# Expert weights of a decoder trunk loaded by halves of the rows for both experts of a pair

## The chip, the cores and the metric

The kernel runs on one core of one Trainium2 chip, in one launch. The metric is the device time of that core in microseconds (us); less is better. The kernel before takes 2008.51 us, the median of three runs (2006.98 to 2011.86).

## The reference

A trunk of two layers over 512 tokens of 1024 float32 numbers. Each layer first mixes (an attention with three branches, a state-space branch, gates and an output projection) and then sends each token through two of 32 experts. An expert is `(silu(x @ w_gate) * (x @ w_up)) @ w_down`, with `w_gate` and `w_up` of 1024 x 512 and `w_down` of 512 x 1024, each 2 MB:

```python
g_sel = argmax(h @ w_rg + b_rg)                     # one of 4 groups of experts
top_p, top_i = top_k(softmax(e_logits[g_sel]), 2)   # two experts in the group
w = g_w * top_p / sum(top_p)
for each expert e, xb its tokens:
    out = (silu(xb @ w_gate[e]) * (xb @ w_up[e])) @ w_down[e]
x = x + sum over both experts of w * out
```

All experts' weights are read in each layer: 96 matrices, 201 MB.

## The kernel before

One program with a stream for each engine; semaphores set the order. A layer has a mixing stage and an expert stage; the diff touches the second alone.

**Pairs.** The 32 experts are taken in 16 pairs. A pair's tokens, 64 places for either expert, are one tile of 128: `gather` (L519) fetches rows of the normalised tokens from `h_rows` in DRAM, `turn_rows` (L1011) transposes them, DVE's `gain_rows` (L1841) scales them into `xg`. A round of 16 pairs serves up to 64 tokens an expert; with these inputs a layer takes one round. `both` (L1018) writes the products of both experts of the pair to one PSUM bank, the first expert's to the upper 64 partitions, the second's to the lower: for each of 8 (for `down`: 4) blocks k of rows, one matmul for each expert. One of its calls shows in the trace as 32 records.

**A pair on TensorE** (`pair`, L1026): wait for the tokens; wait for both gate matrices (`landed`, L1030), 16 products to bank 2, `gate_free`; wait for both up matrices, 16 products to bank 3, `up_free`; transposes of the next pair's tokens; once ACT's silu (L1343) and DVE's product (`gated`, L1852) are done, four transposes to bank 6, which ACT copies to `actT` (L1345); wait for both down matrices, 8 products to bank 4 (`half_done`) and 8 to bank 5 (`down_free`). ACT copies both banks to `yslot` (L1348, L1350), and POOL scatters it to `y_rows` in DRAM (L524).

**Loads.** SP issues 96 loads of 2 MB a layer, one matrix of one expert each (`load`, L632), in the order gate, gate, up, up, down, down of each pair. They go to ten places (`slots`, L167), in turn; two of these are the tiles `hT` and `h`, one is `spare_slot`. On a partition a load is 16 KB in one piece, in DRAM too. Loads 0 and 1 are issued while attention runs, 2 to 5 at its end, 6 and 7 when the output projection is done, 8 and 9 when the first pair's token rows have landed (L658). From load 10 on, `refill` (L665) waits for the products that read the load ten before: that is `gate_free`, `up_free` or `down_free`, each counted once a pair.

**The end of a layer.** The last pair's results aren't scattered: TensorE multiplies `yslot` with a matrix of shares (L1074). When the pair before it has been scattered, SP reads all results back (`ytok`, L680: four loads of 1 MB, 8 KB a partition, to `h` and `hT`); DVE adds them to `x` (L1877, eight operations), then the last pair's (L1884, eight operations). The next layer, or the output, waits for that.

**The start of the expert stage.** ACT writes the normalised tokens to `h_rows` tile by tile (L1166); POOL waits for the last of the four and for the table of places (`table_ready`, L1812) and gathers the first pair's rows (L531). This releases TensorE and loads 8 and 9.

Of the kernel before, what the change touches and what calls it, by code (L numbers as in the profile page):

```python
# [24 lines left out]
P = 128  # L25
# [107 lines left out]
def trunk(nc, a, out):  # L133
    with ExitStack() as ctx:
# [39 lines left out]
        def uses(s):  # L174

            return len(range(s, LOADS, NSLOT))
# [4 lines left out]

        def slot_of(i):

            return slots[i % LOADS % NSLOT].rearrange("p (k n) -> p k n", k=KF if KINDS[i % 6 // 2] == "down" else KD)

        squares = view(100, D)
        xrow = view(96, D)
# [258 lines left out]
        def wait_reg(eng, s, value):  # L446

            eng.wait_ge(s, value)
            eng.sem_inc(tick, 1)
# [118 lines left out]
        def _(sp):  # L568
            for t in range(NT):
                sp.dma_start(x[:, t, :], a["x"][0][P * t:P * t + P, :]).then_inc(x_tile[t], 16)  # L570
            with sp.Fori(0, DEPTH) as l:
# [60 lines left out]
                def load(i, pair):  # L632

                    kind = KINDS[i % 6 // 2]
                    src = a["expert_" + kind][bass.ds(l * NE + 2 * pair + i % 2, 1), :, :]
                    sp.dma_start(slot_of(i), src.rearrange("o (p k) n -> p (o k) n", p=P))\
                      .then_inc(slot_in[i % LOADS % NSLOT], 16)

                def freed(i):
# [25 lines left out]
                def refill(j, base, pair):  # L665

                    i = j % LOADS
                    prev = last_load(i) if j >= LOADS else j - NSLOT
                    wait_reg(sp, freed(prev), base + (prev // 6 + 1))
                    load(i, pair)  # L670

                with sp.Fori(0, nb * (PAIRS // BODY) - 1) as q:
# [1 line left out]
                        refill(j, q * BODY, (q * BODY + j // 6) % PAIRS)  # L674
                for j in range(NSLOT, LOADS):
                    refill(j, earlier + (PAIRS - BODY), PAIRS - BODY + j // 6)
                wait_reg(sp, up_free, earlier + (PAIRS - 1))
                wait_reg(sp, y_out, earlier * 16 + 16 * (PAIRS - 1))
                for t in range(NT):
                    sp.dma_start(ytok[t], y_rows[2 * P * t:2 * P * t + 2 * P, :].rearrange("(p k) d -> p k d", k=2))\  # L680
                      .then_inc(y_tok[t], 16)
                wait_reg(sp, gate_free, earlier + PAIRS)
                leave(sp, left_exp)
            for t in range(NT):
                sp.wait_ge(x_tile[t], 16 * (DEPTH + 1))
# [11 lines left out]
        def _(pe):  # L697
# [308 lines left out]
            def experts():  # L1006
                pe.wait_ge(rounds_ready, 1)
                nb = pe.value_load(rounds[0:1, 0:1], min_val=1, max_val=MAXR)
                earlier = pe.value_load(rounds[0:1, 1:2], min_val=0, max_val=PAIRS * (MAXR - 1))

                def turn_rows():  # L1011
                    for k in range(KD):
                        r = pe.transpose(bank[:, k // 4, P * (k % 4):P * (k % 4) + P],
                                         xrow[:, P * k:P * k + P], ident[:, :])
                        if k % 4 == 3:
                            r.then_inc(xt_done, 1)

                def both(dst, moving, first, cols, n):  # L1018

                    for k in range(n):  # L1020
                        for e in range(2):
                            r = pe.matmul(dst[CAP * e:CAP * e + CAP, :], moving[:, k, CAP * e:CAP * e + CAP],  # L1022
                                          slot_of(first + e)[:, k, cols], start=(k == 0), stop=(k == n - 1))
                    return r

                def pair(pp, base, last):  # L1026

                    it = base + pp

                    def landed(first):  # L1030
                        for i in (first, first + 1):
                            s = i % NSLOT
                            wait_reg(pe, slot_in[s], base * (16 * uses(s) // BODY) + 16 * (i // NSLOT + 1))

                    wait_reg(pe, xg_ready, it * 2 + 3)
                    landed(6 * pp)
                    both(bank[:, 2, :], xg, 6 * pp, slice(0, FF), KD).then_inc(gate_free, 1)
                    landed(6 * pp + 2)
                    both(bank[:, 3, :], xg, 6 * pp + 2, slice(0, FF), KD).then_inc(up_free, 1)
                    if last:  # L1040

                        pe.wait_ge(shares_ready, 1)
                        for t in range(NT):
                            r = pe.transpose(bank[:, 7, P * t:P * t + P], share[:, t, :], ident[:, :])
                        r.then_inc(shares_turned, 1)
                    else:
                        wait_reg(pe, rows_in, it * 16 + 32)
                        turn_rows()
                    wait_reg(pe, act_ready, it + 1)
                    for f in range(KF):  # L1050
                        r = pe.transpose(bank[:, 6, P * f:P * f + P], hid[:, f:FF:KF], ident[:, :])  # L1051
                    r.then_inc(at_done, 1)
                    wait_reg(pe, at_ready, it + 1)
                    landed(6 * pp + 4)
                    for half in range(2):
                        wait_reg(pe, y_ready, it * 2 + (1 + half))
                        r = both(bank[:, 4 + half, :], actT, 6 * pp + 4, slice(512 * half, 512 * half + 512), KF)
                        if half == 0:
                            r.then_inc(half_done, 1)
                    r.then_inc(down_free, 1)  # L1060

                pe.wait_ge(rows_in, 16)
                turn_rows()
                with pe.Fori(0, nb * (PAIRS // BODY) - 1) as q:
                    for pp in range(BODY):
                        pair(pp, q * BODY, False)
                for pp in range(BODY):
                    pair(pp, earlier + (PAIRS - BODY), pp == BODY - 1)

                pe.wait_ge(shares_copied, 1)  # L1070
                for half in range(2):
                    wait_reg(pe, y_ready, earlier * 2 + (2 * PAIRS + 1 + half))
                    for t in range(NT):
                        pe.matmul(bank[:, (2 * t + 4 + half) % 8, :], shareT[:, t, :], yslot[:, 512 * half:512 * half + 512],  # L1074
                                  start=True, stop=True).then_inc(y_near, 1)
# [60 lines left out]
        def _(act):  # L1136
# [125 lines left out]
            for l in range(DEPTH):  # L1262
# [76 lines left out]
                act.sem_inc(y_ready, 2)  # L1339
                act.sem_inc(yslot_free, 1)  # L1340
                with act.Fori(0, nb * PAIRS) as it:
                    wait_reg(act, gate_free, it + 1)
                    act.activation(silu, bank[:, 2, :], ACT.Silu).then_inc(silu_done, 1)  # L1343
                    wait_reg(act, at_done, it + 1)
                    act.activation(actT.rearrange("p a b -> p (a b)"), bank[:, 6, :], ACT.Copy).then_inc(at_ready, 1)  # L1345
                    wait_reg(act, half_done, it + 1)
                    wait_reg(act, yslot_free, it + 1)
                    act.activation(yslot[:, 0:512], bank[:, 4, :], ACT.Copy).then_inc(y_ready, 1)  # L1348
                    wait_reg(act, down_free, it + 1)
                    act.activation(yslot[:, 512:1024], bank[:, 5, :], ACT.Copy).then_inc(y_ready, 1)  # L1350
                leave(act, left_exp)

# [2 lines left out]
        def _(dve):  # L1355
# [52 lines left out]
            for l in range(DEPTH):  # L1408
# [439 lines left out]

                def gated(it):
                    wait_reg(dve, silu_done, it + 1)  # L1850
                    wait_reg(dve, up_free, it + 1)
                    TT(hid, silu, bank[:, 3, :], ALU.mult).then_inc(act_ready, 1)  # L1852

                with dve.Fori(0, earlier + (PAIRS - 1)) as it:
# [3 lines left out]
                        gain_rows(q)  # L1858

                late = Chain(dve, exp_chain)  # L1860
                wait_reg(dve, down_free, earlier + (PAIRS - 1))
                for t in range(NT):
                    for k, dst in enumerate((share, share_b)):
                        late(TS(dst[:, t, :], iota_f[:, :], place[:, B_, t, k:k + 1], w_near[:, t, k:k + 1],
# [49 lines left out]
```

## Time and profile before

| | us |
|---|---|
| median of 3 runs | 2008.51 |
| profiled execution, time | 2007.55 |
| its span | 2005.8 |
| PE busy | 1712.3 (85%) |
| DVE busy | 567.3 (28%) |
| ACT busy | 401.9 (20%) |
| DMA, mean over the span | 247 GB/s |
| mean granted TensorE clock | 0.946 |

Times in the rows are in us from the start of the span. In the chain of waits each piece is what the end waited for at that time. A releaser in brackets is what ended the engine's idle time. A load's landing is the last of its 16 engines' parts. A matmul takes two records here, and the two experts' matmuls overlap, so that 32 records take 7.1 us at the full clock.

### The profile page before, as it was taken

To read this page: it belongs to the slowest core of one execution; us is meant where nothing else is said; L and a number is where in the kernel's file an instruction comes from. 1 tells how busy PE (TensorE), PEld (TensorE's weight loads), DVE (VectorE), ACT (ScalarE), POOL (GpSimd) and SP (SyncE) were. 2 spreads that over 40 slices of the span, in tenths; PEclk is the share of its full clock that TensorE was granted. 3 is DMA by queue.
4 is the path that set the end of the run, shared out by engine and by line. 5 is a ranking of instruction groups with operands and counts; after the bars stand their busy time and mean duration, and the time that the engine had idled before them with its cause. 6 is when DMAs were issued, how large, how long until landed. Compare 5 with 4: busy or idle time off the path is not lost.

```text
span 2005.8 us, 21398 instructions
## 1 busy us (share of the span) xinstructions
PE 1712.3 (85%) x7534; PEld 811.0 (40%) x7534; DVE 567.3 (28%) x1748; ACT 401.9 (20%) x959; POOL 80.7 (4%) x153
## 2 busy tenths in 40 slices
PE   7969899999698778787899698999996988787877
PEld 6644344445333233332367343444452333232332
DVE  4753134524200000000356622345252000000003
ACT  2211334303111111101122113343031111111110
POOL 0000000000010000000000000000000000000000
PEclk9989899999799898999999798999997999998999
DMA  5720110152799999999929110102518999999996
GB/s 156 175 93 22 42 43 22 51 231 86 313 426 427 427 427 427 427 427 427 353 62 229 39 42 22 43 22 100 234 59 340 426 428 427 426 427 427 426 427 289
DMA packets 118707, 496.25 MB, mean 247 GB/s; under 512 B 40884, under 2 KB 77748, under 8 KB 93008
## 3 DMA queue, kind: packets, MB, share of 16 engines
q1 hardware_dynamic: 107968, 474.33, 59.4%
q0 software_dynamic: 8928, 16.39, 2.2%
q10 hardware_dynamic: 1712, 4.20, 0.5%
q8 instruction: 64, 1.05, 0.2%
q14 instruction: 35, 0.29, 0.0%
HBM read 488.99 MB, written 30.41 MB: 259 GB/s over the span
## 4 chain that ended last, share of the span: by engine, by line
PE 56%; DMA 31%; DVE 4%; ACT 4%; SPq 2%; issue 2%; POOL 0%; DVEq 0%; POOLq 0%; ACTq 0%
PE bank L1022 15%; PE bank L737 12%; DMA arena<-in_expert_up 12%; PE bank L716 11%; DMA arena<-in_expert_gate 8%; DMA arena<-in_expert_down 6%; PE bank L933 6%; PE bank L868 2%; DMA h<-in_expert_up 2%; PE bank L890 2%; PE bank L900 2%; PE bank L771 1%; SPq L573 1%; DMA h_rows<-h 1%; PE bank L853 1%
## 5 line engine op out<-in xcount | busy, mean ns | idle before, releaser
L1022 PE MATMUL bank<-arena 128*64 128x512 f32 x2240 | 604.7, 627 | 96.7 <-DMA arena<-in_expert_up 40.8
L1022 PEld LDWEIGHTS bank<-arena 128*64 128x64 f32 x2240 | 210.2, 144 | 367.2 <-issue 367.2
L737 PE MATMUL bank<-hT,arena 128*128 128x512 f32 x512 | 269.7, 625 | 46.2 <-ACT arena L1216 44.8
L1852 DVE TENSOR_TENSOR arena<-arena,bank 128x512 f32<-128x512 f32 x32 | 22.0, 688 | 840.2 <-PE bank L1022 840.2
L1022 PE MATMUL bank<-spare_slot,arena 128*64 128x512 f32 x320 | 155.6, 644 | 36.7 <-DMA arena<-in_expert_gate 14.3
L1022 PE MATMUL bank<-hT,arena 128*64 128x512 f32 x256 | 121.5, 631 | 28.9 <-DMA h<-in_expert_up 18.0
L737 PEld LDWEIGHTS bank<-hT,arena 128*128 128x128 f32 x512 | 84.6, 195 | 106.4 <-ACT arena L1216 55.2
L1022 PE MATMUL bank<-h,arena 128*64 128x512 f32 x256 | 121.8, 632 | 0.0
L933 PE MATMUL bank<-arena,hT 128*128 128x512 f32 x256 | 117.8, 612 | 4.2 <-DVE hT L1726 4.2
L716 PE MATMUL bank<-arena,hT 128*128 128x256 f32 (+1 forms) x512 | 115.5, 386 | 1.8 <-ACT h L1189 1.8
L1684 DVE TENSOR_REDUCE nbias<-bank 128x1 f32<-128x31 f32 (+4 forms) x192 | 63.4, 383 | 176.1 <-PE bank L871 95.9
L716 PEld LDWEIGHTS bank<-arena,hT 128*128 128x128 f32 x512 | 97.0, 191 | 17.0 <-ACT h L1189 2.2
L1343 ACT ACT_TABLE_LOAD x32 | 41.1, 1283 | 291.2 <-PE bank L1022 291.2
L1022 PEld LDWEIGHTS bank<-spare_slot,arena 128*64 128x64 f32 x320 | 45.8, 148 | 129.8 <-issue 129.8
L716 PE MATMUL bank<-arena 128*128 128x512 f32 (+1 forms) x208 | 84.7, 567 | 6.0 <-ACT arena L1193 4.9
L1236 ACT ACTIVATE arena<-bank,nbias 128x31 f32<-128x31 f32 (+4 forms) x192 | 82.6, 439 | 8.1 <-DVE nbias L1684 8.1
L1345 ACT ACTIVATE arena<-bank 128x512 f32<-128x512 f32 x32 | 19.1, 597 | 310.4 <-PE bank L1051 310.4
L1022 PEld LDWEIGHTS bank<-hT,arena 128*64 128x64 f32 x256 | 36.1, 145 | 102.7 <-issue 102.7
L933 PEld LDWEIGHTS bank<-arena,hT 128*128 128x128 f32 x256 | 48.0, 195 | 57.9 <-issue 51.9
L1246 ACT ACTIVATE arena<-bank 128x512 f32<-128x512 f32 (+1 forms) x64 | 38.0, 594 | 154.4 <-PE bank L890 154.4
L890 PE MATMUL bank<-ident,arena 128*128 128x128 f32 (+1 forms) x384 | 62.0, 280 | 1.6 <-DVE arena L1699 0.9
L716 PEld LDWEIGHTS bank<-arena 128*128 128x128 f32 (+1 forms) x208 | 37.5, 185 | 53.6 <-issue 46.8
(345 smaller groups left out, 1604.7 us busy)
## 6 DMA issues: line engine op xcount, KB each, us to landing
arena<-in_expert_gate SPq DMA_DIRECT2D x48, 2048.0 KB, 36.9
arena<-in_expert_down SPq DMA_DIRECT2D x48, 2048.0 KB, 38.9
arena<-in_expert_up SPq DMA_DIRECT2D x44, 2048.0 KB, 36.8
arena<-in_w_in SPq DMA_DIRECT2D x26, 1024.0 KB, 8.4
spare_slot<-in_expert_gate SPq DMA_DIRECT2D x8, 2048.0 KB, 30.8
hT<-in_expert_up SPq DMA_DIRECT2D x8, 2048.0 KB, 36.8
h<-in_expert_up SPq DMA_DIRECT2D x8, 2048.0 KB, 42.3
spare_slot<-in_expert_down SPq DMA_DIRECT2D x8, 2048.0 KB, 37.5
```

What stands on the lines that cost most here:

```text
L716: r = pe.matmul(dst, w, m, start=(i == 0), stop=(i == len(pairs) - 1))
L737: r = pe.matmul(bank[:, FB, :], lhs, rhs, start=(k == 0), stop=last)
L868: pe.matmul(bank[:, i, 0:nk], qT[rows, g, P * qt:P * qt + P], keys[rows, :], start=True, stop=False)
L890: r = pe.transpose(bank[0:w, 4 + kt % 2, P * i:P * i + P], prob[:, n % 2, i, P * kt:P * kt + w], ident[:, :])
L900: r = pe.matmul(bank[DH * j:DH * j + DH, 6, 0:2 * P], v, pT[0:w, c % 4, :].rearrange("p (g j t) -> p j g t", g=2, j=2)[:, j], start=(br == ...
L933: r = pe.matmul(bank[:, c, :], mergedT[:, k, P * t:P * t + P], w_o[:, k, 512 * c:512 * c + 512], start=(k == 0), stop=(k == KD - 1))
L1022: r = pe.matmul(dst[CAP * e:CAP * e + CAP, :], moving[:, k, CAP * e:CAP * e + CAP], slot_of(first + e)[:, k, cols], start=(k == 0), stop=( ...
L1236: act.activation(prob[:, n % 2, i, 0:nk], bank[:, i, 0:nk], ACT.Exp, scale=-1.0, bias=nbias[:, n % 2, i:i + 1], accum_out=rsum[:, n % 2, i ...
L1246: act.activation(pT[0:w, c % 4, :], bank[0:w, 4, :], ACT.Copy).then_inc(evac_act, 1)
L1343: act.activation(silu, bank[:, 2, :], ACT.Silu).then_inc(silu_done, 1)
L1684: dve.tensor_reduce(nbias[:, n % 2, i:i + 1], bank[:, i, 0:nk], AX.X, ALU.min).then_inc(max_ready, 1)
L1852: TT(hid, silu, bank[:, 3, :], ALU.mult).then_inc(act_ready, 1)
```

## The change

A load brings half the rows of one matrix, for both experts of the pair, in place of one expert's whole matrix. The place then holds, on each partition, 8 KB of the first expert and 8 KB of the second (`slot_of`). `both` does half of the blocks k for one load, with both experts in turn as before; TensorE waits for one load, multiplies, reports and waits for the next. `gate_free`, `up_free` and `down_free` count twice a pair, and all that wait for them count so too. For `down`, the first half goes to banks 4 and 5, then the second half to both. Order, number and size of the loads, and the ten places, stay.

```diff
--- before.py
+++ after.py
@@ -181,7 +181,8 @@
 
         def slot_of(i):
 
-            return slots[i % LOADS % NSLOT].rearrange("p (k n) -> p k n", k=KF if KINDS[i % 6 // 2] == "down" else KD)
+            return slots[i % LOADS % NSLOT].rearrange("p (e k n) -> p e k n", e=2,
+                                                      k=(KF if KINDS[i % 6 // 2] == "down" else KD) // 2)
 
         squares = view(100, D)
         xrow = view(96, D)
@@ -632,8 +633,9 @@
                 def load(i, pair):
 
                     kind = KINDS[i % 6 // 2]
-                    src = a["expert_" + kind][bass.ds(l * NE + 2 * pair + i % 2, 1), :, :]
-                    sp.dma_start(slot_of(i), src.rearrange("o (p k) n -> p (o k) n", p=P))\
+                    src = a["expert_" + kind][bass.ds(l * NE + 2 * pair, 2), :, :].rearrange("o (p k) n -> p o (k n)", p=P)
+                    n = KD * FF // 2
+                    sp.dma_start(slot_of(i).rearrange("p e k n -> p e (k n)"), src[:, :, n * (i % 2):n * (i % 2) + n])\
                       .then_inc(slot_in[i % LOADS % NSLOT], 16)
 
                 def freed(i):
@@ -666,7 +668,7 @@
 
                     i = j % LOADS
                     prev = last_load(i) if j >= LOADS else j - NSLOT
-                    wait_reg(sp, freed(prev), base + (prev // 6 + 1))
+                    wait_reg(sp, freed(prev), base * 2 + (prev // 6 * 2 + prev % 2 + 1))
                     load(i, pair)
 
                 with sp.Fori(0, nb * (PAIRS // BODY) - 1) as q:
@@ -674,12 +676,12 @@
                         refill(j, q * BODY, (q * BODY + j // 6) % PAIRS)
                 for j in range(NSLOT, LOADS):
                     refill(j, earlier + (PAIRS - BODY), PAIRS - BODY + j // 6)
-                wait_reg(sp, up_free, earlier + (PAIRS - 1))
+                wait_reg(sp, up_free, earlier * 2 + 2 * (PAIRS - 1))
                 wait_reg(sp, y_out, earlier * 16 + 16 * (PAIRS - 1))
                 for t in range(NT):
                     sp.dma_start(ytok[t], y_rows[2 * P * t:2 * P * t + 2 * P, :].rearrange("(p k) d -> p k d", k=2))\
                       .then_inc(y_tok[t], 16)
-                wait_reg(sp, gate_free, earlier + PAIRS)
+                wait_reg(sp, gate_free, earlier * 2 + 2 * PAIRS)
                 leave(sp, left_exp)
             for t in range(NT):
                 sp.wait_ge(x_tile[t], 16 * (DEPTH + 1))
@@ -1015,28 +1017,29 @@
                         if k % 4 == 3:
                             r.then_inc(xt_done, 1)
 
-                def both(dst, moving, first, cols, n):
-
-                    for k in range(n):
+                def both(dst, moving, i, cols, n):
+
+                    for k in range(n // 2 * (i % 2), n // 2 * (i % 2 + 1)):
                         for e in range(2):
                             r = pe.matmul(dst[CAP * e:CAP * e + CAP, :], moving[:, k, CAP * e:CAP * e + CAP],
-                                          slot_of(first + e)[:, k, cols], start=(k == 0), stop=(k == n - 1))
+                                          slot_of(i)[:, e, k % (n // 2), cols], start=(k == 0), stop=(k == n - 1))
                     return r
 
                 def pair(pp, base, last):
 
                     it = base + pp
 
-                    def landed(first):
-                        for i in (first, first + 1):
-                            s = i % NSLOT
-                            wait_reg(pe, slot_in[s], base * (16 * uses(s) // BODY) + 16 * (i // NSLOT + 1))
+                    def landed(i):
+                        s = i % NSLOT
+                        wait_reg(pe, slot_in[s], base * (16 * uses(s) // BODY) + 16 * (i // NSLOT + 1))
 
                     wait_reg(pe, xg_ready, it * 2 + 3)
-                    landed(6 * pp)
-                    both(bank[:, 2, :], xg, 6 * pp, slice(0, FF), KD).then_inc(gate_free, 1)
-                    landed(6 * pp + 2)
-                    both(bank[:, 3, :], xg, 6 * pp + 2, slice(0, FF), KD).then_inc(up_free, 1)
+                    for i in (6 * pp, 6 * pp + 1):
+                        landed(i)
+                        both(bank[:, 2, :], xg, i, slice(0, FF), KD).then_inc(gate_free, 1)
+                    for i in (6 * pp + 2, 6 * pp + 3):
+                        landed(i)
+                        both(bank[:, 3, :], xg, i, slice(0, FF), KD).then_inc(up_free, 1)
                     if last:
 
                         pe.wait_ge(shares_ready, 1)
@@ -1051,13 +1054,15 @@
                         r = pe.transpose(bank[:, 6, P * f:P * f + P], hid[:, f:FF:KF], ident[:, :])
                     r.then_inc(at_done, 1)
                     wait_reg(pe, at_ready, it + 1)
-                    landed(6 * pp + 4)
-                    for half in range(2):
-                        wait_reg(pe, y_ready, it * 2 + (1 + half))
-                        r = both(bank[:, 4 + half, :], actT, 6 * pp + 4, slice(512 * half, 512 * half + 512), KF)
-                        if half == 0:
-                            r.then_inc(half_done, 1)
-                    r.then_inc(down_free, 1)
+                    for i in (6 * pp + 4, 6 * pp + 5):
+                        landed(i)
+                        for half in range(2):
+                            if i % 2 == 0:
+                                wait_reg(pe, y_ready, it * 2 + (1 + half))
+                            r = both(bank[:, 4 + half, :], actT, i, slice(512 * half, 512 * half + 512), KF)
+                            if i % 2 and half == 0:
+                                r.then_inc(half_done, 1)
+                        r.then_inc(down_free, 1)
 
                 pe.wait_ge(rows_in, 16)
                 turn_rows()
@@ -1339,14 +1344,14 @@
                 act.sem_inc(y_ready, 2)
                 act.sem_inc(yslot_free, 1)
                 with act.Fori(0, nb * PAIRS) as it:
-                    wait_reg(act, gate_free, it + 1)
+                    wait_reg(act, gate_free, it * 2 + 2)
                     act.activation(silu, bank[:, 2, :], ACT.Silu).then_inc(silu_done, 1)
                     wait_reg(act, at_done, it + 1)
                     act.activation(actT.rearrange("p a b -> p (a b)"), bank[:, 6, :], ACT.Copy).then_inc(at_ready, 1)
                     wait_reg(act, half_done, it + 1)
                     wait_reg(act, yslot_free, it + 1)
                     act.activation(yslot[:, 0:512], bank[:, 4, :], ACT.Copy).then_inc(y_ready, 1)
-                    wait_reg(act, down_free, it + 1)
+                    wait_reg(act, down_free, it * 2 + 2)
                     act.activation(yslot[:, 512:1024], bank[:, 5, :], ACT.Copy).then_inc(y_ready, 1)
                 leave(act, left_exp)
 
@@ -1848,7 +1853,7 @@
 
                 def gated(it):
                     wait_reg(dve, silu_done, it + 1)
-                    wait_reg(dve, up_free, it + 1)
+                    wait_reg(dve, up_free, it * 2 + 2)
                     TT(hid, silu, bank[:, 3, :], ALU.mult).then_inc(act_ready, 1)
 
                 with dve.Fori(0, earlier + (PAIRS - 1)) as it:
@@ -1858,7 +1863,7 @@
                         gain_rows(q)
 
                 late = Chain(dve, exp_chain)
-                wait_reg(dve, down_free, earlier + (PAIRS - 1))
+                wait_reg(dve, down_free, earlier * 2 + 2 * (PAIRS - 1))
                 for t in range(NT):
                     for k, dst in enumerate((share, share_b)):
                         late(TS(dst[:, t, :], iota_f[:, :], place[:, B_, t, k:k + 1], w_near[:, t, k:k + 1],
```

## Rows read from the trace of the kernel before

**Rows 1.** The page: how much the core's DMA engines moved, in 40 slices of the span.
```profile
GB/s 156 175 93 22 42 43 22 51 231 86 313 426 427 427 427 427 427 427 427 353 62 229 39 42 22 43 22 100 234 59 340 426 428 427 426 427 427 426 427 289
```

**Rows 2.** The page, section 4: shares of the chain that ended last, by line.
```profile
PE bank L1022 15%; PE bank L737 12%; DMA arena<-in_expert_up 12%; PE bank L716 11%; DMA arena<-in_expert_gate 8%; DMA arena<-in_expert_down 6%; PE bank L933 6%; PE bank L868 2%; DMA h<-in_expert_up 2%; PE bank L890 2%; PE bank L900 2%; PE bank L771 1%; SPq L573 1%; DMA h_rows<-h 1%; PE bank L853 1%
```

**Rows 3.** Chain of waits, experts of the first layer: start, length in us, what.
```profile
525.93 15.83 PE bank L1022 x64
...
947.37 9.87 PE bank L1022 x32
...
980.71 14.02 DMA hT<-y_rows
...
999.96 0.66 DVE x L1884
```

**Rows 4.** Chain of waits, end of the second layer's experts.
```profile
1939.57 43.88 DMA arena<-in_expert_down
...
1983.97 8.70 PE bank L1022 x32
```

**Rows 5.** DVE timeline at both ends: start, us, line, [idle before <-releaser].
```profile
989.44 5.12 DVE L1877 SCALAR_TENSOR_TENSOR x<-h,w_far,x 128x1024 f32<-128x1024 f32 x4 [2.14 <-DMA h<-y_rows]
...
1985.96 5.12 DVE L1877 SCALAR_TENSOR_TENSOR x<-h,w_far,x 128x1024 f32<-128x1024 f32 x4 [3.70 <-DMA h<-y_rows]
1991.00 5.12 DVE L1877 SCALAR_TENSOR_TENSOR x<-hT,w_far,x 128x1024 f32<-128x1024 f32 x4
1996.15 0.69 DVE L1884 TENSOR_TENSOR x<-x,bank 128x512 f32<-128x512 f32 x1
1997.26 4.28 DVE L1884 TENSOR_TENSOR x<-x,bank 128x512 f32<-128x512 f32 x7 [0.43 <-PE bank L1074]
```

**Rows 6.** DMA view of the load issued at 944.05: KB, us to landing.
```profile
arena<-in_expert_down SPq DMA_DIRECT2D x1, 2048.0 KB, 42.9
```

**Rows 7.** DMA view, 560 to 960 us: packets, MB, share of 16 engines.
```profile
DMA packets 15082, 170.81 MB, mean 427 GB/s; under 512 B 3344, under 2 KB 3344, under 8 KB 5094
...
q1 hardware_dynamic: 11219, 163.42, 96.0%
```

**Rows 8.** DMA view, 984 to 990 us, tokens' rows come back (8 KB packets).
```profile
DMA packets 346, 2.54 MB, mean 423 GB/s; under 512 B 40, under 2 KB 40, under 8 KB 40
...
q1 hardware_dynamic: 345, 2.53, 100.5%
```

**Rows 9.** DMA view, 396 to 400 us, halves of w_out's rows (2 KB packets).
```profile
DMA packets 784, 1.59 MB, mean 398 GB/s; under 512 B 6, under 2 KB 6, under 8 KB 784
```

**Rows 10.** DMA view of three loads, issued at 523.12, 535.28 and 535.90.
```profile
h<-in_expert_up SPq DMA_DIRECT2D x1, 2048.0 KB, 13.4
...
spare_slot<-in_expert_down SPq DMA_DIRECT2D x1, 2048.0 KB, 8.3
...
arena<-in_expert_down SPq DMA_DIRECT2D x1, 2048.0 KB, 12.6
```

**Rows 11.** DMA view of the second layer's same places, issued at 1519.92 and 1532.02.
```profile
h<-in_expert_up SPq DMA_DIRECT2D x1, 2048.0 KB, 12.9
...
spare_slot<-in_expert_down SPq DMA_DIRECT2D x1, 2048.0 KB, 8.2
```

**Rows 12.** DMA view of two writes to h_rows, issued at 508.91 and 493.56.
```profile
h_rows<-h ACTq DMA_DIRECT2D x1, 512.0 KB, 9.3
...
h_rows<-h ACTq DMA_DIRECT2D x1, 512.0 KB, 3.1
```

**Rows 13.** Timeline ahead of the first gather.
```profile
515.92 0.23 DVE L1812 TENSOR_SCALAR table<-table 128x128 int32<-128x128 int32 x1
...
519.15 1.23 POOL L521 DMA_INDIRECT arena<-h_rows,table  x1 [434.53 <-DMA h_rows<-h]
```

**Rows 14.** PE timeline, two groups of the last pair, each after a landing.
```profile
1963.35 8.76 PE L1022 MATMUL bank<-arena 128*64 128x512 f32 x32 [2.03 <-DMA arena<-in_expert_gate]
...
1973.73 7.09 PE L1022 MATMUL bank<-arena 128*64 128x512 f32 x32 [1.62 <-DMA arena<-in_expert_up]
```

## The prediction, made before the changed kernel was run

> **What bounds the kernel now.** I read the strip of what the DMA engines moved first [rows 1]: both expert stages, slices 12 to 18 and 32 to 39, stand at 426 to 428 GB/s and nothing else does. Then the shares of the chain [rows 2]: the three expert matrices' DMAs make 26% of it beside 15% for the products of L1022. So in the expert stage loads set the pace; TensorE waits for them. Two things follow. Places that come free earlier are worth something only where DMA engines have nothing queued, and products that begin earlier only where the end waits for products.
>
> Where does the end wait? The chain of the first layer's end goes back from DVE's last additions to the read-back of the tokens' rows at 980.71 [rows 3]. The second layer's shows a down load that lands at 1939.57 + 43.88 = 1983.45 and then 8.70 us of products [rows 4]; the naive reading is that halves save half of that. I therefore looked at DVE beside it [rows 5]. Its eight operations L1877 begin when the first read-back lands, 1985.96, take 10.2 us, and L1884 follows at 1996.15 with next to no gap: only 1997.26 - 1996.15 - 0.69 = 0.42 us of the tail is due to late products. In the first layer DVE begins at 989.44, and from 999.96 on it waits for no product. The read-back stands in SP's queue behind the last load: that one lands at 944.05 + 42.9 = 986.95 [rows 6] and the first read-back 2.5 us later, in the second layer 1983.45 and 1985.96, again 2.5 us, the time that 1 MB takes at 427 GB/s. So each layer ends 2.5 + 10.2 + 5 us after its last load lands (the products run beside that), and the place of the last landing is what the change can move.
>
> **The change part by part.**
>
> *Products by halves.* Same number of matmuls. In the last pair the products end earlier by about half a group, 3.5 us of 7.09 [rows 14], in up and in down alike. All but 0.42 us of it falls under DVE's tail. Worth -0.4 us in the second layer, 0 in the first. The cover is DVE's tail: if the read-back came earlier, this would begin to count.
>
> *The two waits more per group.* Chain pieces hold 64 records in 15.83 us across two such waits [rows 3], with a first group that starts at the low clock; a wait that is already met shows no gap. I take 0; even 0.3 us each would leave a pair at 24 + 2 us against the 6 x 5.2 = 31 us that its loads take.
>
> *Places free by halves: the gap at the start of the stage.* Load 9 is issued at 523.12 and lands 13.4 later, at 536.5; load 10 is issued at 535.28, once all 16 gate products are done, and lands at 543.6; load 11 lands at 548.5 [rows 10]. Loads that are queued land 4.9 us apart, these two 7.1: a gap of 2.2 us. In the second layer it is 1532.02 + 8.2 - (1519.92 + 12.9) = 7.4, a gap of 2.5 [rows 11]. After the change load 10 waits for half the gate products: these start at 525.93, and although their start is at the low clock (64 records in 15.83 us, less 7.1 for the second group, leaves 8.7 for the first), the second half is at the full clock, so the first is done 7.09 / 2 = 3.5 us before the whole. Load 10 is then issued near 531.8, before load 9 is through. The gap closes: -2.2 and -2.5 us, I take -2.35 a layer. Bounds 0 (load 10 is not early enough) and -2.5. After this PE needs less time for a pair than its loads do, the queue grows (at the end a load lands 42.9 us after its issue), and earlier issues change nothing.
>
> *Packets.* A load's 16 KB a partition were one packet and are now two of 8 KB. In 400 us of the stage 163.42 MB took 96.0% of 16 engines [rows 7]: 37.6 engine-us per MB, 0.616 us per 16 KB. The read-back has 8 KB packets: 2.53 MB in 100.5% of 96 engine-us, 38.1 per MB [rows 8]. That is 1.4% more by the shares and 0.95% by the rates (427 against 423). The stretch in which loads queue up is 986.9 - 543.6 = 443 us, 85 loads at 5.2. So +4.2 us a layer by the rates; bounds +2.2 (0.5%, as the views are rounded) and +6.2 (1.4%). It all is on the path, since the last landing sets the end. The Trainium skill, DMA: Bandwidth & Descriptors, "Why small descriptors are slow (HBM only)", gives a fixed cost of about 3 cycles per packet, at its 850 MHz 3.5 ns; 8 packets more per load and engine over 85 loads would be an estimated 2.4 us a layer. The rows give more (0.95% of 616 ns is 5.9 ns a packet), and I go by the rows.
>
> *The write of the last tile to h_rows.* It is issued at 508.91 while loads 6 and 7 run and takes 9.3 us; undisturbed it takes 3.1 [rows 12]. The gather of the first pair follows it at 519.15, though the table was ready at 515.92 + 0.23 = 516.15 [rows 13]. Engines take packets of two queues in turn, as far as the 9.3 us tell, so with 8 KB packets between them the 4 KB packets of the write get through sooner. At most the gather starts 1 us after the table (as it does after the write now), at 517.1: -2.0 us. At least 0: the total work of that moment is the same, and the slowest engine is nearly out of loads when it gets to the write. I take -0.8. The whole stage starts that much earlier. The same skill page, "Queues, rings and completion order", says that an engine goes round its queues packet by packet; the row of 9.3 against 3.1 agrees.
>
> *Issues.* 256 pieces instead of 128 per load may make each of SP's issues longer. The issues of 535.28 and 535.90 are 0.62 us apart, so one takes less than that now; with 5.2 us per load even twice as much is hidden, save ahead of loads 8 and 9: 0, bound +0.4.
>
> Sum a layer: -2.35 - 0.8 + 4.2 = +1.05; two layers +2.1, less 0.4 for the end: **+1.7 us**. On the profiled execution's 2007.55 that is 2009.3; it lies 0.96 below the median of the runs, so 2010.2 as a median. I say 2010. Bounds by these terms: low 2 x (-2.5 - 2.0 + 2.2) - 0.4 = -5; high 2 x (0 + 0 + 6.2 + 0.4) = +13.
>
> **The rivals.**
>
> *Faster (13%).* The packets cost next to nothing, since 16 engines are held by something else than the packet's own overhead, and both starts gain in full: 2 x (-2.5 - 2.0) - 0.4 = -9.4, 1999. If the products' halves also counted in the tail, 3.5 a layer, 1992. For it: the chain of the second layer does name the products. Against it: rows 5, and the 423 against 427.
>
> *Slower (15%).* At any time the engines now read one 8 KB half of each 16 KB, at two places 2 MB apart. If that is slower to read than 16 KB in one piece, the last landing moves by 4.4 us a layer for each per cent. It passes a measurable loss (+6) from 1.4 + 0.3 = 1.7% on, 420 GB/s. The nearest row with halves of rows is w_out's: 2 KB of each 4 KB, 398 GB/s [rows 9], 6.8% below; at that rate it is +32 a layer less 3, +58, 2066. But seven packets more per 16 KB at 5.9 ns each are 41 ns of 616, 6.7%: their number explains it, and nothing is left for the gaps between the pieces. I put this rival's middle at 2018. The skill's same page, "Latency and other measured facts", tells of copies with rows 512 KB to 8 MB apart that fall to half the rate; halving the rate for 443 us a layer would end near 2900. Rows lie 16 KB apart here, only the two experts lie 2 MB apart, and nothing in the trace has such a distance; I leave it 1 of the 15%.
>
> *TensorE's clock (7%).* After 2.03 us of idleness a group took 8.76 us, after 1.62 us 7.09 [rows 14]; 9.87 in another case [rows 3]. The waits before each half could leave TensorE at 1.2 GHz for as long as in the worst group now, 9.87 - 7.09 = 2.8 us more, in several halves. The last down products would then end where they do now or 2 to 3 us later, and DVE's last additions would wait for them: 2012 to 2015. For it: six waits a pair in place of three. Against it: each wait is shorter (5.2 less 3.5 us), and a TensorE that falls behind no longer waits.
>
> **How the numbers follow.** Forecast 65%, faster 13%, slower 15%, clock 7%. A measurement of this kernel tells about 0.3%, 6 us, from no change: 2002.5 to 2014.5. Of the forecast's 65 about 3 lie below (its low end and the runs' spread) and 4 above. Faster by over 0.3%: 0.13 + 0.03 = 0.16. Slower: 0.15 + 0.04 + 0.02 of the clock's = 0.21. The same: 0.63. The range, 2001 to 2021, takes in the forecast's bounds but for the last us or two and the slower case up to 0.6%.
>
> **What would show it.** Right: 49,000 packets of 8 KB in place of 24,600 of 16 KB; the stage's rate at 422 to 425 GB/s; loads 9 and 10 landing 5 us apart; the write of the last tile to h_rows at 7.5 to 9; PE's products of the last pair over 3 to 4 us earlier relative to the last landing, with DVE L1877 still beginning 2.5 us after it. Wrong: a rate of 427 (then faster) or under 421 (slower); a read-back that lands before the last load, or a gap between L1877 and L1884 that a product ends.

## The result, and the profile after

The changed kernel takes 2012.87 us (median of 20 runs, 2008.29 to 2018.35) against 2007.78 for the kernel before (20 runs, 2004.66 to 2011.86): ratio 1.0024, interval 1.0015 to 1.0032. That is 5.1 us more, a loss so small that it is inside what I had called "the same", and inside the range of 2001 to 2021; the forecast of 2010 had 1.7 us of loss. The profiled execution took 2009.47 us with a span of 2007.8, 3.4 us less than the median.

First the strips of the page [rows 1]. Each digit or number is one of 40 slices.

```profile
PEclk9989999999799999999999899999998999999999
...
GB/s 156 176 91 22 39 40 28 38 228 102 335 420 420 422 421 421 420 420 421 353 84 217 51 26 38 43 22 94 231 77 357 421 420 420 421 421 422 420 421 307
DMA packets 143281, 496.21 MB, mean 247 GB/s; under 512 B 40884, under 2 KB 77748, under 8 KB 93008
```

Both expert stages stand at 420 to 422 GB/s where they stood at 426 to 428, and the packets are 24,600 more. The DMA view of 560 to 960 us beside [rows 7]: 421 for 427.

```profile
DMA packets 24673, 168.35 MB, mean 421 GB/s; under 512 B 3270, under 2 KB 3270, under 8 KB 5002
```

The DMA view of single loads (KB, us to landing): load 9 of both layers, issued at 522.58 and 1519.87, load 10, at 531.11 and 1528.10, and the last load, at 952.80 and 1953.99 [rows 6, 10, 11].

```profile
h<-in_expert_up SPq DMA_DIRECT2D x1, 2048.0 KB, 13.0
...
h<-in_expert_up SPq DMA_DIRECT2D x1, 2048.0 KB, 13.3
...
spare_slot<-in_expert_down SPq DMA_DIRECT2D x1, 2048.0 KB, 10.0
...
spare_slot<-in_expert_down SPq DMA_DIRECT2D x1, 2048.0 KB, 10.8
...
arena<-in_expert_down SPq DMA_DIRECT2D x1, 2048.0 KB, 38.5
...
arena<-in_expert_down SPq DMA_DIRECT2D x1, 2048.0 KB, 32.9
```

The same two microseconds, 534 to 536, of the kernel before and of this one (after the engines' busy times: PEclk, DMA share, GB/s):

```profile
534.00:536.00 2.00, 2.00 (x12) 0.63 (x9) 0.00 (x0) 0.98 (x1) 0.00 (x0) 1.00 0.42 164
```

```profile
534.00:536.00 2.00, 2.00 (x12) 0.74 (x10) 0.00 (x0) 1.73 (x2) 0.00 (x0) 1.00 1.01 418
```

The hole ahead of load 10, in which the DMA engines were busy for 0.42 of the time, is filled. Loads 9 and 10 land at 535.6 and 541.1, 5.5 us apart in place of 7.1, and at 1533.2 and 1538.9, 5.7 in place of 7.4. The last load lands at 991.3 and 1986.9. From load 10 to the last it is 450.2 and 448.0 us, where it was 443.3 in both layers.

The last write to h_rows, issued at 509.28, and the first gather [rows 12, 13]:

```profile
h_rows<-h ACTq DMA_DIRECT2D x1, 512.0 KB, 8.4
```

```profile
518.59 1.23 POOL L522 DMA_INDIRECT arena<-h_rows,table  x1 [433.78 <-DMA h_rows<-h]
```

From the write's issue to the gather it is 9.31 us, before 519.15 - 508.91 = 10.24.

The end of the second layer. TensorE (start, us, line, [idle before <-releaser]):

```profile
1972.16 3.65 PE L1024 MATMUL bank<-arena 128*64 128x512 f32 x16 [1.89 <-DMA arena<-in_expert_up]
1977.13 3.65 PE L1024 MATMUL bank<-arena 128*64 128x512 f32 x16 [1.32 <-DMA arena<-in_expert_up]
...
1983.76 7.09 PE L1024 MATMUL bank<-arena 128*64 128x512 f32 x32 [1.26 <-ACT arena L1350]
1990.77 7.13 PE L1079 MATMUL bank<-arena,spare_slot 128*128 128x512 f32 x16
```

and DVE [rows 5]:

```profile
1989.34 5.12 DVE L1882 SCALAR_TENSOR_TENSOR x<-h,w_far,x 128x1024 f32<-128x1024 f32 x4 [7.12 <-DMA h<-y_rows]
1994.38 5.12 DVE L1882 SCALAR_TENSOR_TENSOR x<-hT,w_far,x 128x1024 f32<-128x1024 f32 x4
1999.54 4.87 DVE L1889 TENSOR_TENSOR x<-x,bank 128x512 f32<-128x512 f32 x8
```

The reader is to see two things. TensorE works by halves, at the full clock, and its last down products end at 1990.85, 4.0 us after the last landing instead of 9.2. DVE doesn't use it: it stands idle for 7.12 us until the first read-back lands at 1989.3, again 2.5 us after the last load (1986.9), and then runs 15.1 us with no gap. The chain of waits of the second layer now names that read-back, and no products after the last load:

```profile
1970.89 18.43 DMA h<-y_rows
...
1989.34 1.30 DVE x L1882
```

### The profile page after: what moved, and what is told of

Read it like the earlier page. It is cut to its first block, busy times and chain, and to the rows that moved or that the text cites. A ratio compares the mean times of both kernels' runs of the same rounds, so it can differ in the third digit from the quotient of the medians.

```text
span 2007.8 us, 21508 instructions
## 1 busy us (share of the span) xinstructions
PE 1687.9 (84%) x7534; PEld 800.2 (40%) x7534; DVE 567.1 (28%) x1748; ACT 402.2 (20%) x959; POOL 80.7 (4%) x153
## 4 chain that ended last, share of the span: by engine, by line
PE 50%; SPq 26%; DMA 12%; DVE 5%; ACT 4%; issue 2%; POOL 0%; DVEq 0%; POOLq 0%; ACTq 0%
SPq L638 25%; PE bank L739 12%; PE bank L718 11%; PE bank L1024 9%; PE bank L935 6%; DMA arena<-in_expert_up 4%; DMA h<-in_expert_up 4%; PE bank L870 2%; PE bank L892 2%; PE bank L902 2%; DMA hT<-y_rows 1%; PE bank L773 1%; SPq L574 1%; DMA h<-y_rows 1%; DMA h_rows<-h 1%
## 5 line engine op out<-in xcount | busy, mean ns | idle before, releaser
L1024 PE MATMUL bank<-arena 128*64 128x512 f32 x2240 | 510.8, 604 | 122.6 <-DMA arena<-in_expert_gate 51.2
L1024 PEld LDWEIGHTS bank<-arena 128*64 128x64 f32 x2240 | 185.7, 139 | 431.4 <-issue 430.5
L739 PE MATMUL bank<-hT,arena 128*128 128x512 f32 x512 | 273.9, 633 | 46.2 <-ACT arena L1221 44.8
L1024 PE MATMUL bank<-spare_slot,arena 128*64 128x512 f32 x320 | 78.1, 631 | 29.2 <-DMA spare_slot<-in_expert_gate 11.6
L1024 PE MATMUL bank<-hT,arena 128*64 128x512 f32 x256 | 61.8, 625 | 22.8 <-DMA hT<-in_expert_up 13.0
L1350 ACT ACTIVATE arena<-bank 128x512 f32<-128x512 f32 x32 | 19.1, 597 | 298.8 <-PE bank L1054 298.8
L1024 PE MATMUL bank<-h,arena 128*64 128x512 f32 x256 | 58.2, 594 | 8.2 <-DMA h<-in_expert_up 5.3
L1353 ACT ACTIVATE arena<-bank 128x512 f32<-128x512 f32 x32 | 19.1, 598 | 198.3 <-PE bank L1024 198.3
L1024 PEld LDWEIGHTS bank<-spare_slot,arena 128*64 128x64 f32 x320 | 27.2, 145 | 73.2 <-issue 73.1
```

The source lines that it names most:

```text
L739: r = pe.matmul(bank[:, FB, :], lhs, rhs, start=(k == 0), stop=last)
```

## The experiments

**The loads alone.** The changed kernel, with before's waits and reports:

```diff
-                    for i in (6 * pp, 6 * pp + 1):
-                        landed(i)
-                        both(bank[:, 2, :], xg, i, slice(0, FF), KD).then_inc(gate_free, 1)
...
+                    for kind, freed in enumerate((gate_free, up_free)):
+                        for i in (6 * pp + 2 * kind, 6 * pp + 2 * kind + 1):
+                            landed(i)
+                        for i in (6 * pp + 2 * kind, 6 * pp + 2 * kind + 1):
+                            r = both(bank[:, 2 + kind, :], xg, i, slice(0, FF), KD)
+                        r.then_inc(freed, 2)
```

and so for down.

> The changed kernel's loads, but TensorE waits for both loads of a matrix kind before it multiplies and reports both places free together, as before. Theory (the price is the packets): the stage runs at 421 GB/s as in the changed kernel (427 before), the gap between the landings of loads 9 and 10 opens again from 5.6 to about 7.3 us in both layers, and the time is 3 to 4 us above the changed kernel, 8 to 10 above the kernel before (+0.4 to 0.5%). Rival (the price is that products run by halves, with twice the waits): the time falls back to that of the kernel before, 0 to 2 us above it.

Measured: 2019.09 us, ratio 1.0049 (1.0037 to 1.0062). The DMA view of 560 to 960 us:

```profile
DMA packets 24688, 168.36 MB, mean 421 GB/s; under 512 B 3284, under 2 KB 3284, under 8 KB 5016
```

The issues and landings of this trace put loads 9 and 10 at 6.8 and 7.4 us apart, and load 10 to the last at 449.9 and 449.4 us. So the loads' new form costs about 10 us by itself, as expected, and the products by halves with their earlier reports give back about half of it. The rival, that they are what costs, falls.

**More packets, whole matrices.** The kernel before, with each matrix in four quarters, so that a partition takes 4 x 4 KB (the order of the features in `h`, `g_ffn` and `hid` is changed to match):

```diff
-                    sp.dma_start(slot_of(i), src.rearrange("o (p k) n -> p (o k) n", p=P))\
+                    sp.dma_start(slots[i % LOADS % NSLOT].rearrange("p (h n) -> p h n", h=4),
+                                 src.rearrange("o (h p k) n -> p (o h) (k n)", h=4, p=P))\
```

> The kernel before with its whole-matrix loads, products and waits, but a partition's 16 KB come as four pieces of 4 KB from four quarters of the matrix. Theory: each packet costs a fixed time. With the 8.8 ns that 421 against 427 GB/s gives (1.4% of 616 ns for one packet more), three more per 16 KB are 26 ns: 409 GB/s, 18 us a layer, 2040 to 2045 us in all. With the 5.9 ns of the prediction: 415 GB/s and 2030 us. Rival (the size of a packet doesn't matter, the pairing of experts or the early products do): 427 GB/s and 2008 us.

Measured: 2044.14 us, ratio 1.0174 (1.0159 to 1.0189), at 409 GB/s:

```profile
DMA packets 43089, 163.53 MB, mean 409 GB/s; under 512 B 3207, under 2 KB 3207, under 8 KB 43075
```

No pairing of experts and no early products are in this kernel, only packets (and their places: a partition's four pieces lie 512 KB apart). Load 10 and the last load of the first layer, issued at 533.06 and 974.08:

```profile
spare_slot<-in_expert_down SPq DMA_DIRECT2D x1, 2048.0 KB, 8.0
...
arena<-in_expert_down SPq DMA_DIRECT2D x1, 2048.0 KB, 29.3
```

From load 10 to the last it takes 462.4 and 462.0 us: 18.9 more than before for 85 x 8 x 3 = 2040 more packets on each engine, 9.3 ns a packet. The changed kernel has 680 more and 5.8 us more, 8.5 ns. The 409 GB/s and 2044 us are what 8.8 ns a packet was to give; the prediction's 5.9 ns was to give 415 and 2030.

**The same packets, side by side.** The changed kernel, each load reading one unbroken 1 MB of either expert (the order of the features is changed to match):

```diff
-                    src = a["expert_" + kind][bass.ds(l * NE + 2 * pair, 2), :, :].rearrange("o (p k) n -> p o (k n)", p=P)
+                    src = a["expert_" + kind][bass.ds(l * NE + 2 * pair, 2), :, :].rearrange("o (h p k) n -> h p o (k n)", h=2, p=P)
+                    sp.dma_start(slot_of(i).rearrange("p e k n -> p e (k n)"), src[i % 2, :, :, :])\
...
```

> The changed kernel, but a load's half is one piece of 1 MB in DRAM for each expert (rows 0 to 511 or 512 to 1023, for down 0 to 255 or 256 to 511), so that packets are as many and as large (8 KB) and lie side by side instead of every other 8 KB. Theory (number of packets): 421 GB/s and the changed kernel's time within 1.5 us. Rival (the halves' distance costs part of it, since the read-back's 8 KB packets gave 423): 423 to 427 GB/s, 2 to 5 us below the changed kernel in each layer, 4 to 10 in all.

Measured: 2014.99 us, ratio 1.0034 (1.0021 to 1.0047). That is 0.1%, 2 us, above the changed kernel's ratio, a little over the 1.5 us that the theory allowed, but the intervals overlap, and the 4 to 10 us of gain of its rival are not there.

```profile
DMA packets 24739, 168.35 MB, mean 421 GB/s; under 512 B 3327, under 2 KB 3327, under 8 KB 5078
```

The same 421 GB/s, and 449.9 and 448.1 us. It is the number of packets, not the 8 KB left out between them. The two experts still lie 2 MB apart here; that this distance isn't what costs rests on the kernel with 4 KB packets, which reads one expert at a time and pays 9.3 ns a packet.

**The early refill alone.** The kernel before; only loads 0 and 1 of every 48, four of a layer's 96, bring halves, and their places are reported one by one (`by_half(i)` is `i % LOADS < 2`):

```diff
+                    if by_half(i):
+                        n = KD * FF // 2
+                        src = a["expert_" + kind][bass.ds(l * NE + 2 * pair, 2), :, :].rearrange("o (p k) n -> p o (k n)", p=P)
+                        dst, src = slots[i].rearrange("p (e n) -> p e n", e=2), src[:, :, n * (i % 2):n * (i % 2) + n]
...
```

> The kernel before, with only loads 0 and 1 of every 48 (the gates of pairs 0 and 8) by halves of the rows, and their places freed one by one. Theory: 427 GB/s stays, loads 9 and 10 land 5.6 us apart in place of 7.1 and 7.4, and the time is 2 x 1.7 = 3.4 us below the kernel before (-0.17%). Rival (the early refill is worth nothing, as the queue catches up anyway): the same time as before, within 1 us.

Measured: 2005.28 us, ratio 0.9990 (0.9979 to 1.0000).

```profile
DMA packets 15336, 170.72 MB, mean 427 GB/s; under 512 B 3349, under 2 KB 3349, under 8 KB 5097
```

427 GB/s, loads 9 and 10 land 5.5 us apart in both layers, 444.1 and 443.2 us from load 10 to the last. The landings do what the theory says; the time, 2 us less (0 to 4), agrees with 3.4 and just reaches no change. It is the fastest version tried, and clearly ahead of the changed kernel; whether it is ahead of the kernel before stays just unshown.

**The tail uncovered.** Both kernels without the read-back of the tokens' rows (L680) and without DVE's additions of them (L1877); only the last pair's results reach `x`:

```diff
-                for t in range(NT):
-                    sp.dma_start(ytok[t], y_rows[2 * P * t:2 * P * t + 2 * P, :].rearrange("(p k) d -> p k d", k=2))\
-                      .then_inc(y_tok[t], 16)
...
-                        STT(x[:, t, :], ytok[t][:, k, :], w_far[:, t, k:k + 1], x[:, t, :], ALU.mult, ALU.add)\
-                            .then_inc(comb_step, 1)
```

> The kernel before without the read-back of the tokens' rows and without DVE's eight additions of them (only the last pair's results are added). Theory (DVE's tail covers the products): the end then waits for the last down products, which begin after the last landing; a layer's end comes 9.2 + 7.1 + 0.8 = 17 us after the last landing in place of 18.1, so only 1 to 2 us a layer are saved, 2004 to 2006 us. Rival (the end already waits for the products alone): 2007 to 2008.

> The changed kernel with the same two parts left out. Theory: with DVE's tail gone the halves of the last pair count, about 5 us a layer (products end 4.0 after the last landing in place of 9.2), so that the changed kernel's loss of 5 us turns into a gain: f2 is 3 to 7 us below f1, near 2000 us. Rival (the last pair's halves gain nothing of themselves): f2 is 4 to 6 us above f1, as the changed kernel is above the kernel before.

Measured: before so cut 2008.09 us, ratio 1.0005 (0.9994 to 1.0015); changed so cut 2007.56, 1.0001 (0.9991 to 1.0011). The first isn't what I expected (2004 to 2006), nor is the second (near 2000); as expected is only that the second no longer lies 5 us above its partner. The timelines of the first layer's end, PE and DVE of the kernel before, cut:

```profile
987.54 8.61 PE L1019 MATMUL bank<-arena 128*64 128x512 f32 x32 [1.62 <-DMA arena<-in_expert_down]
996.08 7.13 PE L1071 MATMUL bank<-arena,spare_slot 128*128 128x512 f32 x16
```

```profile
997.24 0.69 DVE L1873 TENSOR_TENSOR x<-x,bank 128x512 f32<-128x512 f32 x1 [11.58 <-PE bank L1071]
1000.75 4.27 DVE L1873 TENSOR_TENSOR x<-x,bank 128x512 f32<-128x512 f32 x7 [2.82 <-PE bank L1071]
...
1005.98 0.75 DVE L1419 TENSOR_SCALAR h<-x,stat 128x1024 f32<-128x1024 f32 x1
```

and of the changed kernel, cut:

```profile
990.05 7.42 PE L1021 MATMUL bank<-arena 128*64 128x512 f32 x32 [1.27 <-ACT arena L1347]
997.40 7.13 PE L1076 MATMUL bank<-arena,spare_slot 128*128 128x512 f32 x16
```

```profile
998.56 0.69 DVE L1878 TENSOR_TENSOR x<-x,bank 128x512 f32<-128x512 f32 x1 [10.04 <-PE bank L1076]
1002.07 4.27 DVE L1878 TENSOR_TENSOR x<-x,bank 128x512 f32<-128x512 f32 x7 [2.82 <-PE bank L1076]
...
1007.66 0.75 DVE L1424 TENSOR_SCALAR h<-x,stat 128x1024 f32<-128x1024 f32 x1
```

Why the first gained nothing: I had taken 0.8 us from the last product to the end. But DVE adds tile by tile, both column halves of one before the next, while TensorE makes all tiles' first halves first. So the second addition waits 2.82 us, and seven of the eight come after it. The tail is 1006.0 - 987.2 = 18.8 us from the last landing without the read-back and 18.9 with it: two chains of nearly the same length stood side by side. With halves the products' chain is shorter: the last load lands at 993.7, and the same step begins 14.0 us later, 4.8 less. In the second layer the span ends 21.6 and 16.3 us after the last landing. So about 5 us a layer appear once DVE's read-back no longer covers them, as expected, and the loss of 0.24% is gone. The expected gain of 3 to 7 us of the second over the first isn't there: the medians differ by 0.5 us, which the spread of the runs can't tell from nothing. In the profiled executions the two mixing stages of the second kernel ran 2.6 and 3.0 us longer than the first's; whether that is chance, or something else takes the rest, is open.

**The write first.** The kernel before, SP waits ahead of loads 6 and 7:

```diff
                 leave(sp, left_mix)
+                sp.wait_ge(h_out, 16 * NT)
                 for i in range(6, 8):
```

> The kernel before, with SP waiting for the last write to h_rows before it issues loads 6 and 7. Theory (the write is held up by the 16 KB packets): the write takes 3 us in place of 9.3, the first gather begins 1 us after the table, at 2 us less than before, and the time is 2 x 2 = 4 us below the kernel before (-0.2%). Rival (the later loads 6 to 9 push the gap further out): the gap between loads 9 and 10 is 0 to 1 us wider and the gain is under 2 us.

Measured: 2014.07 us, ratio 1.0043 (1.0028 to 1.0058): slower, against both theories. The DMA view of the write and of the gather that follows (issued at 510.37 and 518.54), and the chain:

```profile
h_rows<-h ACTq DMA_DIRECT2D x1, 512.0 KB, 2.7
...
arena<-h_rows,table POOLq DMA_INDIRECT x1, 7.9
```

```profile
518.54 7.86 DMA arena<-h_rows,table
...
526.45 1.98 PE bank L1014 x8
```

The write takes 2.7 us and the gather starts 8.17 us after the write's issue in place of 10.24, as meant. But loads 6 and 7, now issued at 513.2, stand ahead of the gather, which takes 7.9 us instead of 3.5. Two us won, 4.4 lost. The wait moved to the next small transfer. Counted from the write's issue, the first gather lands 2.3 us later than before, in the second layer 2.6, and the last load 2.4 and 2.9. That is 5.3 of the 8 us; the rest I can't place.

**Both edits.**

> Both edits to the kernel before together: first gates of pairs 0 and 8 by halves, and loads 6 and 7 after the last write to h_rows. Theory: the gains add, 3.4 + 4 = 7 us, 2000 to 2001 us (-0.37%), at 427 GB/s. Rival (with loads 8 and 9 later, they are what load 10 queues behind, so that the early refill finds no gap): the larger of the two alone, 4 us, 2004.

Measured: 2008.52 us, ratio 1.0013 (1.0002 to 1.0023), against both theory (2000 to 2001) and rival (2004). It is better than the write first alone and worse than the first gates alone. The two effects don't add: 8 us lost and 2 won would be 6, and it is about 2.5; why is not shown. It isn't a better version.

## Why the prediction was right

*In short.* The measured median lies in the range, and the mechanism held: DVE's tail covers the earlier products, the gap at the start closes, and packets cost more than the gap gives. But the loss is 5.1 us where 1.7 was forecast, and of the signs named as right one missed, the rate: 421 GB/s, where 422 to 425 was to be seen.

*What bounds.* Right: the loads set the pace, and the end of a layer follows the last landing by the read-back and DVE's additions, 2.5 us and then at most 0.4 of gap, in both layers of both kernels. The naive reading of the chain, half of 8.70 us saved, would have forecast a gain.

*Products by halves.* Worth 0.4 in the forecast; DVE's run from the first read-back to its end went from 1985.96 to 2001.54, 15.6 us, to 1989.34 to 2004.41, 15.1: 0.5; in the first layer, where the forecast had nothing, 0.3. That DVE covers the rest is shown by the cut kernels. What it covers is more than the 3.5 us of the prediction: the products end 5.2 us sooner after the last landing, as the whole group of before took 8.70 us, partly at 1.2 GHz, and the half that is left runs at 2.4 GHz in 3.65. The extra waits cost nothing that can be seen: a half takes 3.65 us, 32 records 7.09.

*The gap.* Forecast -2.35 a layer, measured -1.6 and -1.7. The hole itself is gone (a DMA share of 1.01 where it was 0.42), yet loads 9 and 10 land 5.5 to 5.7 us apart, not the 4.9 of loads 10 and 11. The first gates alone give the same 5.5. What makes these two landings wider with no engine idle is not shown.

*Packets.* Forecast +4.2 a layer, measured 450.2 - 443.3 = +6.9 and +4.8, mean 5.8; the upper bound was 6.2. This is the term that was mis-sized: I priced a packet at 5.9 ns from the read-back's 423 GB/s and a stage at 427, and it costs 9. The six microseconds of the read-back's view were too few to tell 423 from 421. The shares of the same rows gave 1.4%, which is what came, and I kept them as the bound; the 2.4 us a layer estimated from 3.5 ns a packet was further off. The rival of distant halves fell by the side-by-side kernel. The row of w_out (398 GB/s), from which I took that nothing else was hidden in the price, bears less than I let it: the same four microseconds of the second layer, 1396 to 1400, have 388. One sentence of that rival is to be put right and one to be made more exact. By the sum's own terms a loss of 6 us is reached at 1.4%, 421 GB/s, not at 1.7%. And the Trainium skill, DMA: Bandwidth & Descriptors, "Latency and other measured facts", has half the rate for rows 4 and 8 MB apart only; at 512 KB its copies are nearly at full rate, and at 2 MB they have about three quarters. No run here falls like that: 421 GB/s with experts 2 MB apart.

*The write.* Forecast -0.8, measured -0.9 and -0.8 (1515.41 - 1506.04 = 9.37 against 1515.83 - 1505.71 = 10.12). That the size of the packets beside it does this fits the third size: with 4 KB packets the first layer's write took 7.7 us, after 9.3 and 8.4.

*Issues.* Forecast 0. One issue of SP takes 0.39 us where it took 0.35.

*The sum.* 2 x (-1.65 - 0.85 + 5.8) - 0.5 = +6.1 by landings, against +5.1 by the medians and +1.7 forecast. Taken whole, from the write's issue to the last landing it is +4.0 and +3.1 us, from there to the next layer's norm -0.3 and to the end of the span -1.4: +5.4. The end's 1.4 are DVE's 0.5 and 0.9 of the last store of the output, which lands 2.9 us after its issue instead of 3.8, for a reason that no run shows.

*TensorE's clock.* The rival with 7% went the other way: 0.965 granted on the mean for 0.946, in the expert stages 0.98 for 0.94 and 0.95. The last pair's halves, after waits of 1.3 to 1.9 us, ran at 2.4 GHz, where a whole group after 2.03 had begun at 1.2 [rows 14]. The length of the wait ahead doesn't decide it alone: of the kernel before, the last down products took 8.70 us after a wait of 1.44, and of the changed kernel a half took its 3.65 us after one of 2.50:

```profile
1983.97 8.70 PE L1022 MATMUL bank<-arena 128*64 128x512 f32 x32 [1.44 <-DMA arena<-in_expert_down]
```

```profile
946.17 3.65 PE L1024 MATMUL bank<-hT,arena 128*64 128x512 f32 x16 [2.50 <-DMA hT<-in_expert_up]
```

One difference isn't the change's. The spans of the profiled executions are only 2.0 us apart. The second layer's mixing stage, the same code in both, from the norm of its first tile to the last write to h_rows, took 499.8 us before (1005.9 to 1505.7) and 496.1 after. The windows of 1005 to 1505 us, kernel before, then after (after the engines' busy times: PEclk, DMA share, GB/s):

```profile
1005.00:1505.00 500.00, 457.12 (x2007) 245.54 (x2007) 223.96 (x718) 134.24 (x388) 0.91 (x4) 0.96 0.27 85
```

```profile
1005.00:1505.00 500.00, 453.96 (x2007) 243.81 (x2007) 227.65 (x723) 137.48 (x393) 0.93 (x4) 0.97 0.28 87
```

The stage's length goes with the granted clock, 0.96 and 0.97, and the kernels of the experiments fall into the same two groups: 499.8 to 500.9 us at 0.96 in six of the ten profiles, 496.1 to 497.5 at 0.97 in four; kernels with whole matrices and kernels with halves stand in both. One profiled execution can't tell 5 us; twenty runs can.

## What to carry to other kernels

A load-bound stage pays for each packet: before a transfer is cut so that work can begin on its parts, count the packets per engine and multiply by what one more costs here, then look whether the engine that waits for the parts is on the path at all. Cut only where a queue is empty: halving four loads of 96, of which two meet an empty queue, closed the gap as far as halving all of them did. And a chain of waits names one of several chains; ask at the end of a stage what the other engines wait for, and by how little they lose.

## What was not expected of the hardware

A packet more costs 8.5 to 9.3 ns when 16 engines are busy, about the same for 8 KB and 4 KB packets, and for 8 KB side by side or apart (427, 421 and 409 GB/s for 16, 8 and 4 KB). A small transfer suffers for the large ones issued just ahead of it, a write as well as a gather: a gather of 128 rows takes 3.5 us on empty engines and 7.9 behind two loads of 2 MB. And it suffers less when their packets are smaller: the gathers of 560 to 960 us, with 16, 8 and 4 KB packets beside them,

```profile
arena<-h_rows,slot_tok POOLq DMA_INDIRECT x13, 10.7
```

```profile
arena<-h_rows,slot_tok POOLq DMA_INDIRECT x13, 8.9
```

```profile
arena<-h_rows,slot_tok POOLq DMA_INDIRECT x13, 7.5
```

The 16 engines drift apart while the queue is long: in the kernel before the 16 parts of load 9 of the first layer land within 1.8 us, those of its last load 23.1 to 42.9 us after the issue. A layer waits for the last of them.
